# Scores of a chunked gated recurrence: 16-column sweeps with one reference each, against references at block boundaries of 128, 64 and 32 tokens, the next step's factors made behind the mask

## The reference, cut to what matters

```python
# per chunk: k, v, b = cumulative sum of log f inside the chunk, q
S_new = exp(b_last) * S + einsum('bhsd,bhsv->bhdv', k * exp(b_last - b), v)
A = einsum('bhtd,bhsd->bhts', q * exp(b - b_mid), k * exp(b_mid - b))
A = where(tri, A, 0.0)
o = einsum('bhts,bhsv->bhtv', A, v) + einsum('bhtd,bhdv->bhtv', q * exp(b), S)
```

## Time and profile before

| | us |
|---|---|
| median of 3 runs (2523.38 to 2526.27) | 2525.91 |
| the profiled execution's own time | 2524.84 |
| its span in the trace | 2523.1 |
| PE busy, share of the span | 2291.5, 91% |
| DVE, ACT, POOL busy | 1097.4, 876.4, 247.7 |

### The profile page before, as it was taken

One profiled execution on the slowest core, in us unless ns is written; L12 is line 12 of the kernel. 1 busy time (PEld: TensorE's weight loads), 2 busy tenths in 40 slices (PEclk: granted clock), 3 DMA queues, 4 the chain that ended last, 5 costly groups with the idle time before them and its releaser, 6 DMA issues. The chain is left out here.

```text
span 2523.1 us, 30773 instructions
## 1 busy us (share of the span) xinstructions
PE 2291.5 (91%) x11346; PEld 1753.1 (69%) x11347; DVE 1097.4 (43%) x1970; ACT 876.4 (35%) x1242; POOL 247.7 (10%) x204
## 2 busy tenths in 40 slices
PE   8988899699977899799999799669989999999998
PEld 3576668654464566567666576368878789889898
DVE  2013324430115656366665466353646324442433
ACT  2213322210021455266655465332343222431322
POOL 0002201200000122132222132100000000000000
PEclk9998899699998999899999999879989999999999
DMA  8110115041105689389999699631111222322221
GB/s 346 67 50 34 34 52 199 1 175 67 50 1 228 257 289 338 113 313 334 339 333 330 221 330 342 197 119 68 68 34 67 84 88 80 109 101 84 101 84 67
DMA packets 62210, 390.72 MB, mean 155 GB/s; under 512 B 16240, under 2 KB 16368, under 8 KB 29680
## 3 DMA queue, kind: packets, MB, share of 16 engines
q1 hardware_dynamic: 42768, 355.22, 37.5%
q0 software_dynamic: 19296, 33.62, 5.5%
HBM read 381.94 MB, written 43.52 MB: 169 GB/s over the span
## 5 line engine op out<-in xcount | busy, mean ns | idle before, releaser
L1644 PE MATMUL bank<-moe_work 128*128 128x512 f32 x512 | 235.2, 602 | 1.5 <-ACT moe_work L1291 1.5
L1623 PE MATMUL bank<-moe_gu_high,moe_x_high 128*128 128x512 f32 x512 | 211.1, 412 | 22.8 <-issue 13.1
L1916 DVE TENSOR_TENSOR b_w_rest<-ring,b_w_high 128x2048 fp32r<-128x2048 f32 x63 | 144.4, 2291 | 195.8 <-ACT b_w_high L1911 195.6
L775 PE MATMUL bank<-HT,ring 128*128 128x512 f32 x512 | 222.4, 593 | 0.9 <-DVE mixer_work L586 0.9
L1627 PE MATMUL bank<-moe_gu_high,moe_x_rest 128*128 128x512 f32 x512 | 204.6, 400 | 0.0
L1626 PE MATMUL bank<-moe_gu_rest,moe_x_high 128*128 128x512 f32 x512 | 204.3, 399 | 0.0
L1456 DVE TENSOR_TENSOR moe_gu_rest<-ring,moe_gu_high 128x2048 fp32r<-128x2048 f32 x64 | 143.8, 2288 | 127.4 <-ACT moe_gu_high L1264 127.4
L1456 DVE TENSOR_TENSOR moe_gu_rest<-moe_work,moe_gu_high 128x2048 fp32r<-128x2048 f32 x64 | 143.8, 2288 | 123.5 <-ACT moe_gu_high L1264 123.5
L1911 ACT ACTIVATE b_w_high<-ring 128x2048 fp32r<-128x2048 f32 x63 | 120.2, 1909 | 172.8 <-PE bank L2604 126.8
L775 PEld LDWEIGHTS bank<-HT,ring 128*128 128x128 f32 x512 | 97.2, 191 | 118.8 <-issue 117.3
L2295 PE MATMUL bank<-b_w_rest,b_h_high 128*128 128x256 f32 x608 | 174.7, 287 | 0.0
(11 more groups left out here) (412 smaller groups left out, 4506.7 us busy)
## 6 DMA issues: line engine op xcount, KB each, us to landing
ring<-in_stream_dram SPq DMA_DIRECT2D x122, 1024.0 KB, 4.9
moe_work<-in_experts_dram SPq DMA_DIRECT2D x32, 2048.0 KB
moe_work<-in_experts_dram SPq DMA_DIRECT2D x64, 1024.0 KB
ring<-in_experts_dram SPq DMA_DIRECT2D x32, 2048.0 KB
X<-in_x_dram SPq DMA_DIRECT2D x8, 512.0 KB, 6.1
moe_work<-ffn_sums SPq DMA_DIRECT2D x8, 512.0 KB, 5.4
adarow<-in_rows_dram SPq DMA_DIRECT2D x1, 2048.0 KB, 22.6
h_rows<-moe_work SPq DMA_DIRECT2D x4, 512.0 KB, 23.0
```

Source lines behind the costliest of these rows:

```text
L775: last = mm(bank_of(key)[:, 0:width], w[:, k, half * P:(half + 1) * P], src[:, k, lo:lo + width], start=(k == 0), stop=(k == KD - 1))
L1623: first = mm(banks[2][:, :], xh[:, k, :], wh[h][:, c], start=(k == 0), stop=False)
L1644: last = mm(banks[4 + j][:, :], HDT[o % 2][:, k, :], w[:, k, 512 * j:512 * (j + 1)], start=(k == 0), stop=(k == 1))
L1916: nc.vector.tensor_tensor(WL[u % FEED], raw(u), high_at(u), ALU.subtract).then_inc(s["w_rest"], 1)
```

## The change

The scores of a latent step are no longer made in eight sweeps. Three kinds of square blocks cover the triangle:

- Blocks of 16 columns against the 32 keys of the pair that they stand in: 32 matmuls, weights from a small tile `KO` with three variants of each pair (own reference for the first and the second 16, and the pair's cross term), columns from `QD` as before.
- The two 32 x 32 blocks in each half: 8 matmuls, reference at token 31 (32 backwards) of each 64, factors side by side in `S32`.
- The 64 x 64 block across the halves: 4 matmuls, reference at token 63 (64 backwards), factors in `S64`.

DVE makes all references of a step in four subtractions (`references`), ACT makes seven exponentials (`scaled`), and POOL and DVE multiply by k and q in four and three instructions. `EK` and these factors for step n + 1 are made in step n, right behind the mask (`scans`, `references`, `scale` on DVE, `ends`, `scaled` on ACT). `DEC` gets two buffers, and the exponential for `QE` moves behind the copy `KTs`. The first step's scan and end factor move in front of the second half of `values`. `KK` is laid out by chunk.

Each direction has the same twelve fills. Their places change: one (`mid`) stands between the state product and the output of each step, the others (`last`) behind the output.

The diff, cut to its core:

```diff
+FILL0 = [([("g", 0, 0)], []), ([("g", 0, 1)], [("g", 1, 0)]), ...
+AHEAD1 = [("row", 0, 0), ("row", 0, 1)]
+FILL1 = [([("row", 1, 0)], []), ([("row", 1, 1)], []), ([("row", 2, 0)], [("sp", 0)]), ...
...
-    KM = [grid(part(25088 + 512 * i, 512), 4) for i in range(2)]
+    KO = part(25088, 768).rearrange("p (a b c) -> p a b c", a=16, b=3)
...
@@ block.gpsimd
-                for j in range(NS):
-                    pool.wait_ge(s["e_k"], NS * step + j + 1)
-                    nc.gpsimd.tensor_tensor(km, km, KK[:, :, t * P + lo:t * P + hi], ALU.mult).then_inc(s["k_ready"], 1)
+                pool.wait_ge(s["e_scaled"], 7 * step + 1)
+                nc.gpsimd.tensor_tensor(KO[:, :, 0:3:2, :], KO[:, :, 0:3:2, :], k16, ALU.mult).then_inc(s["k_ready"], 1)
...             (KO[:, :, 1, :], then the key halves of S64 and S32, each behind its exponential)
@@ block.scalar
+            def ends(n):
+                act.wait_ge(s["b_ready"], n + 1)
+                if n:
+                    act.wait_ge(s["kt_done"], n)
+                if n > 1:
+                    act.wait_ge(s["state_ready"], n - 1)
+                for h in range(4):
+                    nc.scalar.activation(EK[:, h, :], BB[:, h, :], ACT.Exp, bias=BB[:, h, end:end + 1], scale=-1.0)
+                nc.scalar.activation(DEC[n % 2][:, :], BB[:, :, end], ACT.Exp).then_inc(s["e_end"], 1)
...
+            def recur(n, mid, last):
...
+                nc.scalar.activation(KTs, grid(banks[6][:, :], 4), ACT.Copy).then_inc(s["kt_copied"], 1)
+                if latent(n):
+                    nc.scalar.activation(QE, BB, ACT.Exp).then_inc(s["e_qe"], 1)
+                if i < 5:
+                    ends(n + 1)
+                    if latent(n + 1):
+                        scaled(n + 1)
+                for key in mid:
+                    fill(key)
...             (copy of the output, then last)
@@ block.vector
+            def references(n):
+                mark(v.tensor_tensor(QD..., b16, b16[:, :, mid:mid + 1].to_broadcast(...), ALU.subtract), "exponent_ready", 4 * step + 1)
+                mark(v.tensor_tensor(KO[:, :, 1, :], b32[:, :, q, mid:mid + 1].to_broadcast(...), b32[:, :, k, :], ALU.subtract), ...)
+                at = 63 if d == 0 else 64
+                mark(v.tensor_tensor(S64, BB, BB[:, :, at:at + 1].to_broadcast([P, 4, P]), ALU.subtract), ...)
+                at = 31 if d == 0 else 32
+                mark(v.tensor_tensor(S32..., b64, b64[:, :, at:at + 1].to_broadcast([P, 8, 64]), ALU.subtract), ...)
...
+            def recur(n, mid, last):
...
+                    mark(v.copy_predicated(AT, mask, grid(banks[4][:, :], 4)), "at_ready", step + 1)
+                    dve.wait_ge(s["e_qe"], step + 1)
+                    mark(v.tensor_tensor(QE, QE, qT..., ALU.mult), "qe_ready", step + 1)
+                if i < 5:
+                    scans(n + 1)
+                    if latent(n + 1):
+                        references(n + 1)
+                    scale(n + 1)
+                for key in mid:
+                    fill(key)
...             (output added, state updated, then last)
@@ block.tensor
+                    for h in range(4):
+                        for j in range(NS):
+                            r, c = 2 * SUB * (j // 2), SUB * (j % 2)
+                            ko = KO[:, 4 * h + j // 2, :, :].rearrange("p b c -> p (b c)")
+                            mm(A[r:r + 32, h, SUB * j:SUB * (j + 1)], ko[:, c:c + 32], QD[:, h, SUB * j:SUB * (j + 1)],
+                               start=True, stop=True)
...
+                    for h in range(4):
+                        mm(A[k, h, q], S64[:, h, k], S64[:, h, q], start=True, stop=True)
...             (S32 likewise for two halves g; then the state product)
+                for key in mid:
+                    fill(key)
+                if lat:
+                    pe.wait_ge(s["at_ready"], step + 1)
+                    pe.wait_ge(s["qe_ready"], step + 1)
```

More of the change, by code:

```diff
@@ L122, in mixer_items @@
         it.add(("fc", 1, h), "act")
-    for r in range(4):
-        for j in range(2):
-            it.add(("row", r, j), "dve")
-    for g in range(4):
-        it.add(("sp", g), "dve")
+    for key in AHEAD1:
+        it.add(key, "dve")
+    for mid, last in FILL1:
+        for key in mid + last:
+            it.add(key, "dve")
     for m in range(4):
@@ L245, in mixer @@
     ADA = tiny(32)
[L246 removed]
+    DEC, SS, SS2 = [tiny(4) for _ in range(2)], tiny(16), tiny(16)
     ST, MV, RS = tiny(24), tiny(8), tiny(4)
@@ L451, in keys @@
-                def keys(first, last):
-                    for j in range(first, last):
-                        lo, hi = (0, SUB * (j + 1)) if d == 0 else (SUB * j, P)
-                        act.wait_ge(s["kmid_ready"], NS * step + j + 1)
-                        km = KM[j % 2][:, :, lo:hi]
-                        nc.scalar.activation(km, km, ACT.Exp).then_inc(s["e_k"], 1)
-                if t >= NC_:
-                    keys(0, 2)
+                nc.scalar.activation(DEC[n % 2][:, :], BB[:, :, end], ACT.Exp).then_inc(s["e_end"], 1)
@@ L463, in recur @@
                 nc.scalar.activation(KTs, grid(banks[6][:, :], 4), ACT.Copy).then_inc(s["kt_copied"], 1)
[L464 to L466 removed]
+                if latent(n):
+                    if step_of(n):
+                        act.wait_ge(s["o_done"], step_of(n))
+                    nc.scalar.activation(QE, BB, ACT.Exp).then_inc(s["e_qe"], 1)
[4 more added lines that the diff above has]
+                for key in mid:
                     fill(key)
[L468 removed]
+                if latent(n) and d == 0:
                     act.wait_ge(s["o_done"], i - 1)
                     nc.scalar.activation(O[:, t - NC_, :], banks[5][:, :], ACT.Copy).then_inc(s["o_copied"], 1)
+                for key in last:
+                    fill(key)
             gates(0)
+            ends(0)
             for n in range(6):
[L474 to L476 removed]
+                recur(n, *FILL0[n])
             act.wait_ge(s["ln_var"], 1)
@@ L640, in recur @@
+            def recur(n, mid, last):
+                d, i, t = STEPS[n]
+                lat, step = latent(n), step_of(n)
+                if lat:
+                    dve.wait_ge(s["a_done"], step + 1)
                     if step:
@@ L858, in fill, with recur @@
                     last.then_inc(s_full, 1)
-            def recur(n, filler):
+            def recur(n, mid, last):
                 d, i, t = STEPS[n]
-                lat = t >= NC_
-                step = 4 * d + i - 2
+                lat, step = latent(n), step_of(n)
                 pe.wait_ge(s["kend_ready"], n + 1)
```

225 lines of the change are left out of this document (134 added, 91 removed).

## The result

The changed kernel takes 2578.55 us (median of 4 runs, 2575.43 to 2583.41) against 2526.02 us for the kernel before in the same comparison: ratio 1.0212, 95% interval 1.0191 to 1.0233. It is slower by 2.1%, clear of no change. Forecast were 2425 us and a range of 2412 to 2452. The profiled execution has a span of 2579.7 us.

A forecast was written before the change was run, and what follows sets the result against it. PE bounds the kernel; time is won in the recurrence's waits and half-clock work. Savings of 50.2 forwards and 55.2 backwards (105.4 us), less 4.6 for one clock fall, take 2525 to 2425 us; range 2412 to 2452.

The forecast's parts named there:

- The step that failed: Phases outside the recurrence, experts included: stand behind a barrier and only shift; everything behind 518 us unchanged, no cost.
- The scores, 4.1 us a step: Latent-step scores on PE: 2.72 us narrow matmuls, 0.66 for 64 x 64, 0.68 for 32 x 32; upper bound 5.4.
- rival 4: Scores and clock: clock never falls, short matmuls to different output rows overlap, up to 8 us more; 2412 us, chance 0.05.
- Forwards: Forward direction of the recurrence: PE's own work sums to 117.9 us against 168.05, 50.2 less.
- Backwards: Backward direction of the recurrence: PE's own work sums to 79.7 us against 134.93, 55.2 less.
- the state of step n is wanted 5 us into step n + 1: PE's wait for the state update between steps: listed among the other waits, none given a cost.
- Rival 2: Backward steps: factors late, DVE's cycle bounds through products stretched beside POOL or slow `KO` patterns; 2430 to 2450 us, chance 0.13.
- DVE is nearly full but not the bound: Backward cycle: DVE needs 14.5 us against PE's 15.4, so PE sets the pace.
- The clock: Latent steps: PE's clock falls in one of eight, costing 4.6 us; 33 to 43 us if all fall.
- Rival 1: PE's clock falls in most latent steps, as short matmuls do not hold it; 2434 to 2463 us, chance 0.24.
- Factors: Early factors: ready in time, backwards by about 1 us; POOL 3.8 us, DVE products about 1.6 us beside POOL.
- rival 3: POOL's four multiplies delay the scores; some 21 us for 1280 elements makes it slower, 2526 us or more; chance 0.02.

The follow-up runs named there:

- the run with 111: Changed kernel plus 111 instructions' worth of further TensorE waits (222, two packed into each) at the expert phase's start: 2403.77 us, ratio 0.9526.
- the run with alternating banks: Changed kernel with 116 wait instructions; turned keys and state product share one PSUM bank, the next step's the other: 2402.84 us, ratio 0.9518.
- the one with `QE` on GpSimd: Changed kernel with 116 wait instructions and PSUM banks alternating by step, decayed-query product moved from VectorE to GpSimd: 2407.46 us, ratio 0.9531.
- The pair of runs with the loop of 1745: Changed kernel with longer skipped code in the expert loop (1745 places) and further waits ahead: 2421.77 us starting at 218, 2558.26 us starting at 30.
- the loop of 2045: Changed kernel with four skipped stretches of the expert loop each 90 places longer, 221 wait instructions at the expert phase's start: 2627.04 us.

## Why the prediction was wrong

**The step that failed** stands in its first paragraph: "The other phases stand behind a barrier and only shift", and again in its last: "everything behind 518 us should be unchanged". Work shifts in time, but code shifts in place, and the expert loop was near the edge: on my count it may start up to 111 places into a packet and stood at 95 to 110. This step is worth +170.2 us. What the runs show in its place: the code that the change adds moves the loop over the bound, 145 waits alone do the same to the kernel before, and 111 waits undo it. Without this step the sum would have been a forecast of 2425 for 2403.8 measured (the run with 111), below the range's lower end of 2412: the range was wrong there as well, by the next point. (7.0 of that run's 119.4 us lie in the expert phase, 770.0 for 777.0, where seven runs alike in it are spread over 6.6; they are no gain of the recurrence.)

**The scores, 4.1 us a step.** They are 1.75. Of the three terms, the 64 x 64 blocks (0.66 forecast, 0.61 to the next) and the 32 x 32 ones (0.68 forecast, 0.38 to the next) are near; the 32 narrow matmuls were put at 2.72 and took 0.76 to the next, because those to different rows overlap. That makes 2.35 us in eight steps, 18.8 us. The first sweep of the earlier trace rows could not show it: all its matmuls write the same rows. With them in that order it is 1.90 us even so, under the 2.72. This was rival 4, to which I gave 0.05 and at most 8 us for the overlap.

**Forwards** 117.9 forecast; less 4 x 2.35 it is 108.5, and measured are 108.41. Turn, state product, fill and output were right within 0.2 us each.

**Backwards** 79.7 forecast; less 9.4 it is 70.3, measured 76.92. Here a new wait took part of the gain back, PE before the state product for VectorE's state update: 5.0 us in four places, and 1.2 more for the first state. The prediction had said "the state of step n is wanted 5 us into step n + 1"; with shorter scores it is wanted 2.3 us in, and VectorE's cycle of 14.2 to 15.0 us (its state updates L727 begin at 345.50, 359.66, 374.62 and 389.56) is longer than PE's of 12.85 (342.36 to 355.21 with alternating banks, where it waits for nothing). VectorE's cycle had been put at 14.5 and was right; PE's had been put at 15.4. Rival 2 named VectorE as the bound, by its products; the run with alternating banks and the one with `QE` on GpSimd show that it is. "DVE is nearly full but not the bound" held only for scores of 4.1 us.

**The clock.** One step of eight was forecast to fall, 4.6 us. One did, behind the longest of those waits (L975 in 2.04 for 1.16 us at 376.26), and cost about 1.4 us; the mean clock of the directions is 1.00 and 0.98. Rival 1 did not come. At 448.5 in the kernel before, from which the prediction took that short matmuls do not hold the clock, PE had been idle since 447.8, so that row says as much for the idle time.

**Factors.** Made early, they are there in time at every turn of a latent step; undoing that costs 54.5 us in the two directions. VectorE's products beside GpSimd took 1.65, 1.10 and 0.83 us, as forecast from the earlier trace rows; GpSimd's took 1.76, 1.17, 1.17 and 0.90, 5.0 us for the 3.8 estimated by size, so rival 3's 21 us were far off.

In all, 105.4 − 4.6 = 100.8 us of gain were forecast and 117.6 found, beside a loss of 170.2 that was not in the sum.

## What to carry to other kernels

A change that adds instructions on an engine also moves every loop behind it in that engine's code. Before saying that a later phase only shifts, count the loop's instructions from the records (weight loads and matmuls apart, skipped branches included), and compare the packets of the instruction queue and the "issue" waits before and after; a loop that is fetched on every turn shows every packet that it touches, and one more, on each turn (nine here). If a good change comes out slower in a phase that it does not touch, shift that code by some instructions before giving the change up: 111 waits turned 1.0212 into 0.9526 here.

## What the runs showed of the hardware

- TensorE keeps a loop only if it lies, with its skipped code, within seven packets of 256 instructions: loops of 1681 and 1745 places were fetched once or on every turn by their start, as in the table; over the bound, the phase took 917 to 947 us for 770 to 783, with 116 to 119 packets more. Why seven, when the 128 KiB in the Trainium skill (Runtime: NRT & Kernel Launch, Instruction fetch mechanics) are eight, is not shown. The packets give a hint. The pair of runs with the loop of 1745 has 18 and 135 in the expert phase: 117 more, 13 times 9, for a loop that lies in eight. For the loop of 2045, which lies in nine, it is 151 less an estimated 21 for its code read once (17 and 1080 further places), 13 times 10. So each turn reads one packet beyond the loop; seven kept and one read ahead would make eight.
- An instruction of two waits whose semaphore has been reached costs TensorE 0.109 us.
- 32 matmuls of 32 output rows by 16 columns take 0.83 us if neighbouring pairs go to different rows, and 1.90 if eight in a row go to the same.
- The totals of kernels alike but for the recurrence differed by up to 6.6 us in the expert phase, so gains of 2 to 3 us in the recurrence are seen in its stretch, not in the total.
